# Attention scores on VectorE: distance, score, slope and minimum in one instruction from the second group of heads on

## The reference, cut to what matters

```python
s = jnp.einsum(..., q, k) * scale - slopes * dist      # slopes = 2 ** (-8 (h + 1) / 16)
p = masked_softmax(s, dist >= 0)                        # fully masked rows give zeros
o = jnp.einsum(..., p, v)
o = gate_c * o_c + gate_s * o_s + gate_w * o_w          # then o @ w_out
```

## Time and profile before

| | |
|---|---|
| three runs | 779.17, 781.89, 781.61 us; median 781.61 |
| span of the profiled execution | 774.2 us |
| median less that span | 7.4 us |
| TensorE matmul busy | 745.7 us, 96% of the span |
| VectorE busy | 521.3 us, 67% |
| ScalarE busy | 380.7 us, 49% |
| POOL busy | 71.4 us, 9% |
| mean granted TensorE clock | 0.991 of full |

### The profile page before, as it was taken

How to read it: one execution, slowest core, us unless ns; L and a number is a source line. 1 busy time by engine, 2 the same in 40 slices (tenths; PEclk the granted TensorE clock), 3 DMA queues, 4 the chain that set the end, 5 groups by cost and what they waited for, 6 DMA issues and landing times.

```text
span 774.2 us, 18656 instructions
## 1 busy us (share of the span) xinstructions
PE 745.7 (96%) x7876; PEld 700.5 (90%) x7876; DVE 521.3 (67%) x742; ACT 380.7 (49%) x584; POOL 71.4 (9%) x52
## 2 busy tenths in 40 slices
PE   8999999998999999999999999989999999999997
PEld 6988888998878999999999989866579999999997
DVE  4896986776453788785555678686857977764441
ACT  6657453121443645544444435767866544443441
POOL 0000005190130000000000010024320000000000
PEclk9999999999999999999999999998999999999999
DMA  9954330000111589967666554400045665676651
GB/s 294 273 172 130 108 110 3 5 3 2 57 56 45 164 216 250 241 193 221 197 195 194 170 164 115 159 1 1 1 139 164 193 209 178 204 212 194 192 164 54
DMA packets 110893, 109.23 MB, mean 141 GB/s; under 512 B 7120, under 2 KB 109776, under 8 KB 110704
## 3 DMA queue, kind: packets, MB, share of 16 engines
q1 hardware_dynamic: 110832, 108.34, 47.1%
HBM read 107.28 MB, written 1.05 MB: 140 GB/s over the span
## 4 chain that ended last, share of the span: by engine, by line
PE 83%; DVE 8%; ACT 3%; SPq 2%; DMA 1%; issue 1%; POOL 1%; ACTq 0%; DVEq 0%; POOLq 0%
PE ps L451 63%; PE ps L667 4%; DVE SB L2053 1%; DMA raw<-in_rwkv_w_in 1%; DVE Gs L1711 1%; PE ps L815 1%; ACT SB L1458 1%; PE ps L764 1%; PE ps L566 1%; PE ps L978 1%; DVE nmx L2059 1%; PE ps L758 1%; DVE LT L1737 1%; PE ps L549 1%; POOL t L2122 1%
## 5 line engine op out<-in xcount | busy, mean ns | idle before, releaser
L1526 DVE TENSOR_TENSOR wlo<-raw,whi 128x1024 fp32r<-128x1024 f32 x188 | 226.1, 1225 | 88.4 <-ACT whi L1120 86.1
L1120 ACT ACTIVATE whi<-raw 128x1024 fp32r<-128x1024 f32 x124 | 130.4, 1059 | 127.8 <-PE ps L451 122.4
L451 PE MATMUL ps<-xh,whi 128*128 128x256 f32 x896 | 178.6, 281 | 2.6 <-DVE xl L2081 1.0
L451 PE MATMUL ps<-xl,whi 128*128 128x256 f32 x896 | 175.7, 278 | 0.0
L451 PE MATMUL ps<-xh,wlo 128*128 128x256 f32 x896 | 175.6, 278 | 0.0
L451 PEld LDWEIGHTS ps<-xh,whi 128*128 128x128 f32 x896 | 135.7, 188 | 6.7 <-issue 4.1
L451 PEld LDWEIGHTS ps<-xl,whi 128*128 128x128 f32 x896 | 135.5, 188 | 0.0
L451 PEld LDWEIGHTS ps<-xh,wlo 128*128 128x128 f32 x896 | 135.4, 188 | 0.0
L1355 ACT ACTIVATE whi<-raw 128x1024 fp32r<-128x1024 f32 x64 | 68.0, 1063 | 78.0 <-PE ps L451 59.4
L451 PE MATMUL ps<-hh,whi 128*128 128x256 f32 x512 | 99.8, 276 | 0.0
L451 PE MATMUL ps<-hh,wlo 128*128 128x256 f32 x512 | 99.8, 276 | 0.0
(11 more groups left out here) (309 smaller groups left out, 988.0 us busy)
## 6 DMA issues: line engine op xcount, KB each, us to landing
raw<-in_mlp_w SPq DMA_DIRECT2D x128, 512.0 KB, 4.4
raw<-in_rwkv_w_in SPq DMA_DIRECT2D x24, 512.0 KB, 5.0
raw<-in_nsa_w_in SPq DMA_DIRECT2D x20, 512.0 KB, 4.5
raw<-in_rwkv_w_out SPq DMA_DIRECT2D x8, 512.0 KB, 3.5
raw<-in_nsa_w_out SPq DMA_DIRECT2D x8, 512.0 KB, 3.5
cw<-in_nsa_cmp_w SPq DMA_DIRECT2D x4, 512.0 KB, 9.4
cst<-in_consts SPq DMA_DIRECT2D x1, 1047.0 KB, 11.2
xtok<-in_x SPq DMA_DIRECT2D x2, 512.0 KB, 4.3
```

Source lines behind the costliest of these rows:

```text
L451: last = mm(ps[:, bank0 + m, 0:T], w[:, slot, c0:c0 + P], x_[:, kk, :], start=(kk == 0 and n == 0), stop=(kk == ktiles - 1 and n == 2))
L1120: A(whi[:, s, :], raw[:, s, :], ACT.Copy).then_inc(hi_ready, 1)
L1526: v.tensor_tensor(wlo[:, slot, :], raw[:, slot, :], whi[:, slot, :].bitcast(f32), ALU.subtract)\
```

## The change

From group 1 on, the slope is taken out of the scaling: queries of head h carry 1 / slope (with a minus sign that moves from the score into the gain of the keys), so that distance plus score, times slope, is what was there before. One VectorE instruction for each head does the sum, the product and the minimum over the row. The reduction of those 12 items goes. Group 0 keeps its steps, with the sign changed. The compressed scores use the same stretched queries, so all heads get a product with `fac` (nrq for heads 0 to 3, minus slope for the others) and a difference. Two small copies fill `fac`; the copy that makes `rqT` scales by a tile of constants instead of a number; the gain for the keys takes two instructions; the constants gain 17 columns.

```diff
+    cols["nslope"] = np.broadcast_to(-np.array(SLOPES)[None, :], (P, H))
+    cols["nstretch"] = -1.0 / np.array(SLOPES)[i % H][:, None]
...
+    fac = place("fac", [P, TT, H], misc + 6528)
...
-            A(rqT[:, :], ps[0:H, 4, 0:T], ACT.Copy, scale=-1.0).then_inc(sem("rqT_ready"), 1)
+            A(rqT[:, :], ps[0:H, 4, 0:T], ACT.Copy, scale=cc("nstretch", 0, H)).then_inc(sem("rqT_ready"), 1)
...
-            step(v.tensor_scalar(tiny[:, 4:7], par[:, pcol["kn0"]:pcol["kn0"] + 3], pv("qn"), None, ALU.mult))
+            step(v.tensor_scalar(tiny[:, 4:5], pv("kn0"), pv("qn"), None, ALU.mult))
+            step(v.tensor_scalar(tiny[:, 5:7], par[:, pcol["kn1"]:pcol["kn1"] + 2], pv("qn"), -1.0, ALU.mult, ALU.mult))
...
             v.reciprocal(nrq[:, :, :], nrq[:, :, :]).then_inc(sem("nrq_ready"), 1)
+            step(v.tensor_copy(fac[:, :, 4:H], cc("nslope")[:, 4:H].unsqueeze(1).broadcast_to([P, TT, H - 4])))
             dve.wait_ge(sem("nrq_ready"), 1)
+            step(v.tensor_copy(fac[:, :, 0:4], nrq[:, :, 0:4]))
...
-                step(v.tensor_tensor(Sc[:, :, 0:4, 0:NB], raw_[:, :, 0:4, 0:NB],
-                                     nrq[:, :, 0:4].unsqueeze(3).broadcast_to([P, TT, 4, NB]), ALU.mult))
-                step(v.tensor_tensor(Sc[:, :, 4:H, 0:NB], raw_[:, :, 4:H, 0:NB], adc[:, :, 4:H, 0:NB], ALU.add))
+                step(v.tensor_tensor(Sc[:, :, :, 0:NB], raw_[:, :, :, 0:NB], fac[:, :, :].unsqueeze(3).broadcast_to([P, TT, H, NB]), ALU.mult))
                 settle()
-                step(v.tensor_tensor(Sc[:, :, 0:4, 0:NB], adc[:, :, 0:4, 0:NB], Sc[:, :, 0:4, 0:NB], ALU.subtract))
+                step(v.tensor_tensor(Sc[:, :, :, 0:NB], adc[:, :, :, 0:NB], Sc[:, :, :, 0:NB], ALU.subtract))
...
+                def score(i):
+                    return ps[:, 2 * (n % 2) + i % 2, (i // 2) * T:(i // 2) * T + w]
+
+                if j > 0:
+                    for i in range(4):
+                        step(v.tensor_tensor_reduce(SB[n % 4][:, i, 0:w], d, score(i), SLOPES[4 * j + i], FAR, ALU.add, ALU.min,
+                                                    nmx[:, n % 4, i:i + 1]))
+                    settle()
+                    dve.sem_inc(sem("s_read"), 1)
+                    dve.sem_inc(sem("mx_ready"), 1)
+                    return
                 for i in range(4):
-                    step(v.scalar_tensor_tensor(SB[n % 4][:, i, 0:w], d, qsl[:, q, i:i + 1] if j == 0 else SLOPES[4 * j + i],
-                                                ps[:, 2 * (n % 2) + i % 2, (i // 2) * T:(i // 2) * T + w], ALU.mult, ALU.subtract))
+                    step(v.scalar_tensor_tensor(SB[n % 4][:, i, 0:w], d, qsl[:, q, i:i + 1], score(i), ALU.mult, ALU.add))
                 settle()
                 dve.sem_inc(sem("s_read"), 1)
-
-                if j > 0:
-                    v.tensor_reduce(nmx[:, n % 4, :], SB[n % 4][:, :, 0:w], AXX, ALU.min).then_inc(sem("mx_ready"), 1)
-                    return
```

More of the change, by code:

```diff
@@ L97 @@
                ("lmask64", C), ("eye64", C), ("hsel", 3 * H - 2), ("chunk", T),
-               ("dist", P * TT * (TT + 1) // 2), ("adc", TT * H * 16), ("unit", P), ("shift", P), ("last", 2)):
+               ("dist", P * TT * (TT + 1) // 2), ("adc", TT * H * 16), ("nslope", H), ("nstretch", 1), ("unit", P), ("shift", P), ("last", 2)):
     CONST_AT[_n] = (_o, _w)
```

## The result

| | before | changed |
|---|---|---|
| median of four runs | 780.39 us (777.0 to 781.89) | 796.8 us (796.61 to 800.13) |
| span of the profiled execution | 774.2 us | 798.0 us |
| ratio, 95% interval | | 1.0216 (1.0173 to 1.026) |

A forecast was written before the change was run, and what follows sets the result against it. TensorE, busy 96% of the span, was taken as the bound, with VectorE and ScalarE on the chain in attention. Span 774.2 - 3.0 (rounds) + 0.4 (compressed scores) = 771.6; time 781.61 - 2.6 = 779.0 us, range 776.2 to 783.6.

The forecast's parts named there:

- 17 more columns of constants in an early load ... nothing: Constants' load near 447 us: TensorE is busy there without a gap, so the added columns cost nothing.
- the one for the other side: VectorE's wide items: fused instruction at scan's rate plus full read, 0.855 us each; 786.5 us, slower; chance 0.05.
- The fused instruction: VectorE, attention stage: four fused instructions take 1.9 us per wide item, against 2.78 before with the reduction.
- g: Saving per wide item on VectorE, taken as 0.9 us; from 0.5 up the total gain stays 3.0 us.
- Rivals 1 to 3: Fused instruction at scan's rate: 782.6, chance 0.08; main and read one after the other: 780.6, 0.15; both: 786.5, 0.05.
- rival 5: Attention stage: a new bound (ScalarE, or a stall beside POOL) eats the earlier minimum; about 781.5 us; chance 0.05.
- The rounds: Three four-item rounds of the attention chain: each shrinks from 12.51 to about 11.5 us, ScalarE limiting; 3.0 us gained.
- The compressed scores: VectorE before item 3's soft: difference of 480 columns, streamed only after POOL's end, adds 0.4 us to the chain.
- The clock: Slow stretch at the lower clock, about 521 to 527 us in the attention stage, costing some 2.5 us.
- The rival that the change would make it vanish: Rival 4, attention stage: the slow clock stretch disappears, 776.5 us, faster; chance 0.07.
- The base: Starting time 781.61 us, median of three runs; span 774.2, the last 7.4 us lying around it, untouched.

The follow-up runs named there:

- the kernel before + 64: The kernel before with 64 unused bytes placed behind the constants, so every tile placed after them lies 64 bytes higher, no instruction changed: 798.27 us, ratio 1.023.
- the changed kernel at the old addresses: The changed kernel with tile tiny moved into unused bytes behind ri, so later tiles lie as in the kernel before: 773.77 us, then 779.32 us in more rounds.
- the kernel before with 192, 576 and 32 bytes: The kernel before with that many unused bytes behind the constants (32 without rounding later starts to 64): 794.22, 801.5 and 792.97 us.
- the changed kernel at distance 192: The changed kernel with 192 unused bytes behind the constants, moving operands 192 bytes behind a multiple of 512 from the weights: 779.84 us, ratio 0.9995.
- all tiles + 64: The kernel before with all tiles 64 bytes higher, weights and moving operands alike, their distance kept: 780.33 us, ratio 1.0009.
- weights + 64: The kernel before with whi and wlo 64 bytes higher and every moving operand where it was: 795.76 us, ratio 1.0181.
- distance 320: The changed kernel with 320 unused bytes behind the constants, distance 320 bytes behind a multiple of 512: 791.07 us (two runs), ratio 1.0161.

## Why the prediction was wrong

The measured 796.8 us lies above the whole range of 776.2 to 783.6. **The step that failed** is "17 more columns of constants in an early load ... nothing". It priced the load and not the place. The 64 bytes cost a ratio of 1.023 by themselves, all of the loss, and they act on the bound itself: TensorE's large matmuls are on the chain for two thirds of the span, and their starts came 120.0 ns apart instead of 113.3. No row of the trace before shows the price, but its two rates (117.8 and 113.3 for the same instruction at the full clock) were there and weren't looked for. They say that something beside the clock and the shape sets the rate.

**The rivals** all had their place on VectorE, in the attention stage or in the clock. The measured time lies above even the one for the other side (786.5), by a mechanism that was none of them.

**The fused instruction.** Taken: 0.42 us from start to start, 1.9 per wide item. Measured: 0.34 and 1.45. The size of this term was off, and it made no difference, as the prediction says, since from g = 0.5 ScalarE limits. Rivals 1 to 3 fall: neither the scan's rate nor a full read. So does rival 5: the gain did arrive, as the next paragraph shows. The Trainium skill's statement that an operation with an accumulator output is two instructions ("VectorE: DVE Perf Modes", on two Vector instructions with no wait between them) is what the trace shows. The prediction also cited that page's rule that the next operation waits for an empty pipeline, and set it against starts 0.33 apart. The same section goes on to say that an operation that isn't held starts earlier, and the fused instructions' starts, 0.34 apart for 0.42, agree with that sentence.

**The rounds.** Forecast 11.5 us for a round, ScalarE without a gap, 3.0 us in all. Measured 11.48, gapless, and 3.0: compare the kernel before + 64 with the changed kernel at the old addresses, of which neither has a lower clock in these parts. From the kernel before + 64:

```profile
512.35 0.39 PE ps L1033 x2
...
534.38 0.66 PE ps L1013 x4
...
572.10 2.99 PE ps L452 x23
```

572.10 - 534.38 = 37.72, against 562.05 - 527.37 = 34.68. Right, mechanism and size. The other traces without a lower clock in this part say the same: 37.7 us for the kernel before with 192, 576 and 32 bytes, 34.6 for the changed kernel at distance 192 and for the second trace of the changed kernel at the old addresses, a gain of 3.0 to 3.1.

**The compressed scores.** Forecast +0.4, the difference about 1.0 us long beside POOL. Measured from the turn of the queries' roots to the compressed transposes: 527.37 - 505.01 = 22.36 against 534.38 - 512.35 = 22.03, +0.33. POOL and VectorE in the changed kernel at the old addresses:

```profile
517.10 1.04 POOL L2185 TENSOR_TENSOR SB<-SB,cof 128x512 f32<-128x512 f32 x1 [3.58 <-DVE cof L2085]
```

```profile
517.62 1.03 DVE L2019 TENSOR_TENSOR Sc<-cst,Sc 128x480 f32<-128x480 f32 x1
```

It ended 0.51 after POOL, its 480 columns' time. Where POOL was through earlier (the changed kernel itself), it took 0.66. Right.

**The clock.** The slow stretch is no fixed price of the place. The kernel before + 64 has none in the attention stage, and the item-to-item code there is that of before; its 37.72 us against 40.41 give the price of the stretch of 6.8 us, 2.7 us (2.5 were put down). With one of 3.4 us (all tiles + 64, weights + 64) the same part took 39.3 us, a price of 1.6. The rival that the change would make it vanish is not borne out: it comes and goes between executions of the same instructions.

**The base.** The text subtracted from 781.61 and took 7.4 us to lie around the span. In the changed kernel's profiled execution it is 800.13 - 798.0 = 2.1, and in the other runs the same. So the profiled execution of before was, by that, one of some 776 us, at the low end of what the kernel does: beside the later kernels, the lowest of its runs was 773.5 us, and the medians were 780 to 784. The range was built on a scatter of 2.7 us; the two rates alone give up to 4.5 ns x 3024 matmuls = 14 us between executions in the MLPs, by estimate. An execution with the slower rate in both would then take some 790 us; the one profiled at distance 320, 788.0 us, had it in most of both.

## What to carry over

A tile that grows moves all that is placed behind it. Before a result is put down to an edit, run the old kernel at the new addresses and the new one at the old: here the move is worth +18 us, and the edit -2.7 us in the attention stage, which the traces show and the whole time doesn't resolve (1.000, 0.9962 to 1.0039). Only such a pair of kernels tells them apart. And in a trace, compare the distance from start to start of the commonest instruction between two kernels, and between stages of one, before any chain is read. For this shape, keep the distance from weight tiles to moving operands at an odd multiple of 64 bytes, until something better is known. It buys the chance of 113.3 ns and not the certainty: the slower draw, 117.8, is nearly the 118.7 of the remainders 128 and 384.

## What the runs showed of the hardware

Matmuls of fp32r with weights 128 x 128 and 256 moving columns, back to back with their weight loads at the full clock, have four steady rates, 113.3, 117.8, 118.7 and 120.0 ns (and 118.3 at an odd multiple of 32 bytes), set by the remainder of the distance between the two operands' addresses in SBUF. All six kernels at remainders 0, 128 and 384 kept their one rate in every large stage; the exceptions are two short products at 120.0 instead of 118.7.

At odd multiples of 64 bytes there are two rates, and the change from one to the other comes only at a pause. In the seven traces there are 208 unbroken rows of 12 to 1536 of these matmuls (starts less than 128 ns apart), and not one changed its rate within. In the kernel before, the first change stands at 41.5 us, where two starts lie 290 and 195 ns apart; 117.8 before it, 113.3 behind it. In the changed kernel at distance 320, the change in the first MLP stands where TensorE waited for wlo:

```profile
319.22 0.30 PEld L455 LDWEIGHTS ps<-xh,whi 128*128 128x128 f32 x2 [0.19 <-DVE wlo L1530]
```

A pause need not bring a change: at distance 192 three of them left the 113.3 ns as it was. What chooses between them is open, and so is the mechanism: that the reads of weights and moving columns meet in the memory would fit, but is argued, not shown. Only this shape was tried; the 64 x 64 products (L667) and the fp32 ones (L566, 6.87 and 6.88 us) didn't change.

In the changed kernel at distance 192 the first MLP waited for its weights three times, with 0.4, 1.1 and 1.0 us from one start to the next. Its chain of waits:

```profile
269.81 0.88 PE ps L495 x4
...
284.20 10.43 DMA raw<-in_mlp_w
...
320.88 9.40 DMA raw<-in_mlp_w
...
332.77 114.52 PE ps L455 x1008
```

These are transfers of about 10 us, where the median is 4.4 us on the page of before. From 270.69 (the end of L495) to 447.29 the matmuls took 176.60 us with 113.3 ns between them, against 174.10 in the kernel before: so the faster rate isn't the whole of a stage's time either. At distance 320 TensorE waited twice for 0.2 us in the same stage, the first time at 113.3 ns; the kernel before, at 113.3 ns throughout, didn't. Whether the faster rate brings such waits, or the transfers were slow for a reason of their own, these executions don't tell.
